# Attention heads with V and the weights split, and the denominators summed on GpSimd

## The reference, cut to what matters

```python
def attend(q, k, v):
    s = jnp.einsum('bqhd,bkhd->bhqk', q, k).astype(jnp.float32) * (MLA_QK ** -0.5)
    p = jax.nn.softmax(s, axis=-1).astype(v.dtype)
    return jnp.einsum('bhqk,bkhd->bqhd', p, v)
# 8 heads, 96 numbers of q and k, 64 of v per head, all float32
# context: 128 queries on their own 128 keys
# latent:  1024 queries on 1024 latent keys and 128 keys of a cache
```

## Time and profile before

| | |
|---|---|
| median of 3 executions | 3778.74 us (3765.2 to 3779.14) |
| the profiled execution | 3774.8 us, its span 3773.0 us |
| PE busy | 3434.7 us, 91% of the span |
| DVE busy | 1973.3 us, 52% |
| ACT busy | 870.4 us, 23% |
| POOL busy | 312.4 us, 8% |
| attention heads of the first layer | about 590 to 961 us of the span |
| attention heads of the second layer | about 2421 to 2793 us |

### The profile page before, as it was taken

The page is one execution under the profiler, slowest core; times in us unless marked ns, Lnnn a source line. Parts: engine busy times, 40 slices in busy tenths (PEclk is TensorE's granted clock), DMA queues, the critical chain, the costliest instruction groups (busy, mean ns, idle before and its releaser), DMA issues. The chain is left out here.

```text
span 3773.0 us, 47227 instructions
## 1 busy us (share of the span) xinstructions
PE 3434.7 (91%) x18786; PEld 3134.0 (83%) x18786; DVE 1973.3 (52%) x3110; ACT 870.4 (23%) x1244; POOL 312.4 (8%) x260
## 2 busy tenths in 40 slices
PE   5985978989979999999989897789998999999998
PEld 4984866666869999999979886566677999999998
DVE  6785535565155665556455755455633543443343
ACT  3112224444231111101131223344432111111100
POOL 1000012221210000000010000212211100000000
PEclk8996568999989999999999966799999999999999
DMA  6500010001112212222121000000011111111011
GB/s 255 159 23 7 16 44 4 2 2 62 45 59 82 79 61 94 73 78 67 45 83 45 28 3 13 4 4 2 11 73 34 45 49 40 44 38 51 33 44 51
DMA packets 44645, 184.32 MB, mean 49 GB/s; under 512 B 5424, under 2 KB 8944, under 8 KB 43120
## 3 DMA queue, kind: packets, MB, share of 16 engines
q1 hardware_dynamic: 37616, 157.53, 11.9%
q0 software_dynamic: 6912, 25.17, 2.3%
HBM read 168.09 MB, written 14.59 MB: 48 GB/s over the span
## 5 line engine op out<-in xcount | busy, mean ns | idle before, releaser
L988 PE MATMUL ps<-a_hi,gu_hi 128*128 128x384 f32 x2112 | 712.0, 337 | 29.8 <-DVE a_lo L1448 23.9
L988 PE MATMUL ps<-a_hi,gu_lo 128*128 128x384 f32 x2112 | 710.2, 336 | 0.0
L988 PE MATMUL ps<-a_lo,gu_hi 128*128 128x384 f32 x2112 | 710.1, 336 | 0.0
L988 PEld LDWEIGHTS ps<-a_hi,gu_hi 128*128 128x128 f32 x2112 | 400.2, 189 | 36.2 <-issue 17.6
L988 PEld LDWEIGHTS ps<-a_lo,gu_hi 128*128 128x128 f32 x2112 | 400.2, 189 | 0.0
L988 PEld LDWEIGHTS ps<-a_hi,gu_lo 128*128 128x128 f32 x2112 | 400.0, 189 | 0.0
L1793 DVE TENSOR_TENSOR at<-ps,sg 128x384 f32<-128x384 f32 x132 | 73.3, 555 | 546.0 <-ACT sg L1320 546.0
L1017 PE MATMUL ps<-g_hi,d_hi 128*128 128x384 f32 x1056 | 354.3, 335 | 4.3 <-DVE g_lo L1795 4.3
L1017 PE MATMUL ps<-g_lo,d_hi 128*128 128x384 f32 x1056 | 354.2, 335 | 0.0
L1017 PE MATMUL ps<-g_hi,d_lo 128*128 128x384 f32 x1056 | 353.9, 335 | 0.0
L909 PE MATMUL ps<-pt,va 128*128 128x512 f32 (+1 forms) x608 | 307.1, 596 | 3.1 <-DVE ya L1726 3.1
(11 more groups left out here) (252 smaller groups left out, 5005.3 us busy)
## 6 DMA issues: line engine op xcount, KB each, us to landing
f_raw<-wgu SPq DMA_DIRECT2D x88, 512.0 KB, 4.6
diag<-wada_c POOLq DMA_DIRECT2D x48, 512.0 KB, 3.8
f_raw<-wdn SPq DMA_DIRECT2D x44, 512.0 KB, 4.6
w_raw<-win SPq DMA_DIRECT2D x32, 512.0 KB, 3.6
wada_z<-wada_b SPq DMA_DIRECT2D x24, 512.0 KB, 4.0
spill<-z SPq DMA_DIRECT2D x2, 4608.0 KB
z<-spill SPq DMA_DIRECT2D x2, 4608.0 KB, 13.7
w_raw<-wout SPq DMA_DIRECT2D x16, 512.0 KB, 3.5
```

Source lines behind the costliest of these rows:

```text
L988: mm = MM(ps[:, 2 * (v % 2) + part, 0:BLK], w, a[:, k, b * BLK:(b + 1) * BLK], start=(k == 0 and j == 0), stop=(k == KC - 1 and j == 2))
```

## The change

The product with V becomes two fp32r matmuls a step. V is split into a high and a low half, which stand side by side as the 128 weight columns: `va` is now [keys, 2, 64]. The exponentials are split too. ACT takes each exponential twice, rounded into `ph` and in f32 into `pf`, and DVE makes `pl` = `pf` - `ph` (`low_weights`). PE multiplies both `ph` and `pl` by `va`. The bank then holds the part from V high in its lower half and that from V low in its upper half. ACT copies the upper half to `t64` (`lower_half`), and DVE adds the two into `tsum`, which keeps two heads, one above the other (`both_halves`).

The ones are gone from `va`. POOL adds up `pf` over the key tiles instead (`accumulate`, 16 additions a head), and once for a pair of heads PE sums over the keys with plain f32 matmuls on ones (`denominators`). DVE inverts them on all 128 partitions (`inverses`, `inverse0`), POOL multiplies (`divided`), ACT rounds (`yhigh`), and POOL makes `a_lo` (`low`).

Further: the context step moves from first to last of the 19; the maxima have no low part any more (`low_rows` and its semaphore are gone); there are 3 max units a step from step 7, where there were 4 from step 6; ACT loads one table that serves the exponential and the logarithm; the low part of V is made on POOL (`low_values`); the residual comes back from HBM in two transfers; and the hardware loops over heads are written out.

```diff
-                MM(ps[:, 6 + (e + o) % 2, 0:n], va[e][:, kt0, :], pt[:, s % 3, 0:n], start=(kt0 <= 1),
+                    pe.wait_ge(at_ph.sem, at_ph.at(l, g + 1))
+                    MM(ps[:, bank, 0:n], va[h % 2][:, kt, :, :], ph[:, g % 3, 0:n], start=first, stop=False)
+                    pe.wait_ge(at_pl.sem, at_pl.at(l, g + 1))
+                    MM(ps[:, bank, 0:n], va[h % 2][:, kt, :, :], pl[:, g % 3, 0:n], start=False,
...
-        S_TRQ, S_TRK, S_PQ, S_PK, S_MAX, S_ROOT, S_ROW = 0, 2, 4, 5, 6, 9, 14
+        S_TRQ, S_TRK, S_VAL, S_PQ, S_PK, S_SUM, S_ROOT, S_INV, S_MAX, S_ROW = 0, 2, 3, 4, 5, 6, 7, 8, 7, 16
...
+                def denominators(h, o, bank):
+                    if o == 2:
+                        pe.wait_ge(at_pf.sem, at_pf.at(l, STEPS * (h + 1)))
+                        sums, dst = [pf0[:, e, :] for e in range(2)], slice(SEQ, 2 * SEQ)
+                    else:
+                        pe.wait_ge(at_acc.sem, at_acc.at(l, 16 * h + 8 * (o + 1)))
+                        sums, dst = [acc[:, e, o, :] for e in range(2)], slice(0, 512)
...
+                    for e in range(2):
+                        mm = MM(ps[DH * e:DH * e + DH, bank, dst], ones[:, 0:DH], sums[e], start=True, stop=True)
...
+                    if h % 2 and st == 13:
+                        denominators(h, 0, o_bank(h, 0))
+                    if h and h % 2 == 0 and st in (3, 4):
+                        denominators(h - 1, 5 - st, o_bank(h - 1, 2))
...
+                        if n == 16 and k == 2:
+                            denominators(H - 1, 2, o_bank(H - 1, 2))
+                            denominators(H - 1, 1, o_bank(H - 1, 1))
...
+                def exponentials(g):
+                    h, st = GLOBAL[g]
+                    n, src = PARTS[at_steps[st][0]][1], 3 + g % 3
+                    act.wait_ge(at_st.sem, at_st.at(l, g + 1))
+                    if g >= 3:
+                        act.wait_ge(at_pv.sem, at_pv.at(l, g - 2))
+                    A(ph[:, g % 3, 0:n], ps[:, src, 0:n], ACT.Exp, scale=SCALE_A).then_inc(at_ph.sem, 1)
...
+                            act.wait_ge(at_acc.sem, at_acc.at(l, acc_after(*GLOBAL[g - 3])))
+                        act.wait_ge(at_pl.sem, at_pl.at(l, max(g - 2, 0)))
...
+                    A(dst, ps[:, src, 0:n], ACT.Exp, scale=SCALE_A).then_inc(at_pf.sem, 1)
...
+                def low_weights(g):
...
+                    TT(pl[:, g % 3, 0:n], src, ph[:, g % 3, 0:n].bitcast(F32), ALU.subtract).then_inc(at_pl.sem, 1)
...
-                    link(V.reciprocal(rec[0:DH, 0:n], ps[DH:P, bank, 0:n]))
-                    TT(ya[half, (e + o) % 2, 0:n], ps[0:DH, bank, 0:n], rec[0:DH, 0:n], ALU.mult).then_inc(at_y.sem, 1)
+                    TT(tsum[half, q0:q0 + n], ps[0:DH, o_bank(h, o), 0:n], t64[0:DH, 0:n], ALU.add).then_inc(at_ts.sem, 1)
...
+                def accumulate(g):
...
+                    pool.wait_ge(at_pf.sem, at_pf.at(l, g + 1))
+                    before = pf[:, (g - 1) % 3, :] if kt == 2 else acc[:, h % 2, o, :]
+                    G.tensor_tensor(acc[:, h % 2, o, :], before, pf[:, g % 3, :], ALU.add).then_inc(at_acc.sem, 1)
...
+                nc.scalar.preload_act_table_set("natural_log_exp_and_others")
```

More of the change, by code:

```diff
@@ new lines, in inverse0, with inverses @@
+                def inverse0(h):
+                    pair = h // 2
+                    dve.wait_ge(at_den.sem, at_den.at(l, 3 * pair + 2))
+                    if pair:
+                        dve.wait_ge(at_ya.sem, at_ya.at(l, 3 * pair - 1))
+                    V.reciprocal(rec0[:, :], ps[:, o_bank(h, 2), SEQ:2 * SEQ]).then_inc(at_rec.sem, 1)
+                def inverses(h, o, bank, first, last):
+                    k = 3 * (h // 2) + (1, 3)[o]
+                    dve.wait_ge(at_den.sem, at_den.at(l, k))
+                    if k > 1:
+                        dve.wait_ge(at_ya.sem, at_ya.at(l, k - 2 if o else k - 1))
+                    for i in range(first, last):
+                        ins = V.reciprocal(rec[:, i * P:(i + 1) * P], ps[:, bank, i * P:(i + 1) * P])
+                    if last == 4:
+                        ins.then_inc(at_rec.sem, 1)
@@ L1743, in _ @@
                 pointwise_low(0)
-                split(0, 0)
+                low_q(0)
+                low_k(0)
                 pointwise_low(1)
-                max_rows(0, 0, True)
-                low_rows(0, 0)
+                for un in range(UNITS):
+                    if un == 6:
+                        sums(1)
+                    if un == 20:
+                        inverse(1)
+                    maximum(0, un)
                 if l == 0:
@@ L1953, in _ @@
                 pool.wait_ge(at_tab.sem, at_tab.at(l, 1))
                 first(0)
+                low_values(0)
                 first(1)
[L1956 to L1962 removed]
@@ L1963, in _ @@
-                head(H - 1, 1, H // 2 - 1, False)
-                pool.wait_ge(at_done.sem, at_done.at(l, 3 * H))
+                pool.wait_ge(ckv_out.sem, ckv_out.at(l, 48))
+                for g, (h, st) in enumerate(GLOBAL):
+                    accumulate(g)
+                    if h + 1 < H and st == 4:
+                        low_values(h + 1)
+                    if h + 2 < H:
+                        if st == 9:
+                            pool.wait_ge(at_rope.sem, at_rope.at(l, h + 2))
+                            normalise_q(h + 2)
+                        if st == 10:
+                            normalise_k(h + 2)
+                        if st == 11:
+                            by_cosine()
+                        if st == 12:
+                            by_sine()
+                        if st == 13:
+                            turned()
+                    if h and h % 2 == 0:
+                        pair = h // 2 - 1
+                        if st == 1:
+                            divided(pair, 0)
+                        if st == 5:
+                            low(pair, 0)
+                        if st == 6:
+                            divided(pair, 2)
+                        if st == 7:
+                            divided(pair, 1)
+                        if st == 14:
+                            low(pair, 2)
+                        if st == 15:
+                            low(pair, 1)
+                    if h == H - 1 and st in (8, 11):
+                        w_low(16 + st // 11)
@@ L1965, in _ @@
+                divided(H // 2 - 1, 0)
+                low(H // 2 - 1, 0)
+                divided(H // 2 - 1, 2)
+                divided(H // 2 - 1, 1)
+                low(H // 2 - 1, 2)
+                low(H // 2 - 1, 1)
                 for n in range(18, 24):
```

509 lines of the change are left out of this document (276 added, 233 removed).

## The result

The changed kernel takes 3852.94 us (median of four, 3851.08 to 3857.84), the kernel before in the same session 3774.69 (four, with the three shown above). The ratio is 1.0213, with a 95% interval of 1.0188 to 1.0237: 78 us slower, where +53 had been forecast. The profiled execution has a span of 3852.8 us against 3773.0.

A forecast was written before the change was run, and what follows sets the result against it. PE was taken to bound the kernel, with DVE taking over in the max-unit steps. Terms of 12 + 5 + 9 + 2 - 1.5 = 26.5 us a layer gave +53 on 3778.7, 3832 us; range 3745 to 3925.

The forecast's parts named there:

- the likeliest case: Whole kernel: DVE's subtractions and POOL's additions collide as forecast, 3832 us, span 3795 to 3865, chance 0.50.
- PE's work falls by 5.4 us a head: Attention heads: cheaper products with V less the added denominators, 87 us over 16 heads if PE stayed the bound.
- DVE becomes the bound of the unit steps: Steps with three max units: subtraction and maxima cost DVE 2.2 us against PE's 1.7 us.
- the walk: Time sum through an odd middle head from its transpose of q: 52.0 us against 50.9 before.
- The collision costs 1.75 us a pair: DVE's subtraction and POOL's addition, both with two SBUF inputs, don't overlap: 1.65 to 1.92 us a pair, taken as 1.75.
- Heads 6 and 7: Last two heads of a layer: 41.4 us against 36.5, and 36.2 against 27.3; +5 and +9 us.
- Heads 0 to 5: Six heads of a layer, odd ones 52.0 us, even ones from 2 on 54.7: 317.4 against 305.2, +12 us.
- The clock rival: More waits in heads bring PE's lower clock: 32 us in all, 3865 us, up to 3925; chance 0.15.
- Denominators: Plain f32 matmuls on PE, 0.87 us per 512 columns: 3.9 us a pair of heads, 2.0 a head.
- The last pair's cover: Output projection's first chunk: seven eighths, some 13 us, cover a chain of about 12; no cost, or a few us.
- No collision: Short DVE and POOL operations slip past each other: 8 us less a layer, 3762 us (3745 to 3785), chance 0.20.
- PE stays the bound: Heads: POOL's additions lag within the buffers, DVE's waits vanish, 87 us of PE work go: 3690 us, chance 0.15.

The follow-up runs named there:

- tiny_both: Changed kernel with POOL's additions and DVE's subtractions both cut to 8 of 512 columns: 3727.07 us, ratio 0.9879.
- psum_sub: Changed kernel with DVE's subtraction reading the scores in PSUM instead of the f32 exponentials in SBUF (result meaningless): 3770.9 us, ratio 0.9992.
- pe_extra: Changed kernel with the first score matmul of steps 7 to 15 of each head done twice: 3856.07 us, ratio 1.0216.
- sum_high: Changed kernel with f32 exponentials written back to PSUM for DVE's subtraction, and POOL summing the rounded exponentials instead: 3773.28 us, ratio 0.9998.
- tiny_inv: Changed kernel with the four reciprocals at the end of heads 3, 5 and 7 cut from 128 to 8 columns: 3854.84 us, ratio 1.0207.
- sums_later: Changed kernel with the sums of squares, their root and inverse, and POOL's following preparation two steps later: 3850.34 us, ratio 1.0202.

## Why the forecast held, and where its sizes were off

3852.94 lies in the likeliest case's own span, 3795 to 3865, in its upper part, and the kernel is slower, as forecast. The mechanism was right. The 3832 is nearer than its parts deserve: six heads were put 22 us a layer too short in the first layer, heads 6 and 7 together 4 us too long. Step by step:

**PE's work falls by 5.4 us a head: the price held, half of the gain could not be had.** The product's two matmuls start 0.23 us apart, as taken; PE in head 2 of after:

```profile
703.39 0.40 PE L959 MATMUL ps<-ph,va 128*128 128x512 f32 x1
703.62 0.40 PE L961 MATMUL ps<-pl,va 128*128 128x512 f32 x1
```

But tiny_both, with the additions and subtractions almost away, gains 46 us of the 87. That the rest stays in the hand-overs between the engines, the chain that the prediction names as the third part of a head, is argued and not shown.

**DVE becomes the bound of the unit steps, at 2.2 us and 2.6 with the collisions: held.** DVE in head 2 of after:

```profile
731.03 1.44 DVE L1782 TENSOR_TENSOR pl<-pf,ph 128x512 fp32r<-128x512 f32 x1
732.39 1.47 DVE L1770 TENSOR_REDUCE pmx<-ps 128x1 f32<-128x384 f32 x3
733.79 0.88 DVE L1782 TENSOR_TENSOR pl<-pf,ph 128x512 fp32r<-128x512 f32 x1
734.59 1.47 DVE L1770 TENSOR_REDUCE pmx<-ps 128x1 f32<-128x384 f32 x3
```

and POOL beside it:

```profile
731.88 2.24 POOL L2019 TENSOR_TENSOR qk<-qk,small 128x960 f32<-128x960 f32 x1
```

Five such steps from 731.03 to 744.09 take 2.61 us each, the forecast's 22 us for 8.3 of them. One piece of this is not the collision: a DVE addition that the walk had left out stands among them.

```profile
735.99 0.67 DVE L1791 TENSOR_TENSOR tsum<-ps,t 64x512 f32<-64x512 f32 x1
```

The subtraction varies between 0.88 and 1.81 us here, as it meets POOL or not; the three maxima, which read PSUM, take 1.47 us whatever POOL does. (The prediction reads this out of the earlier trace rows, but no instruction there has a PSUM input; it is this row and psum_sub that show it.) pe_extra shows the other half: PE had room.

**The collision costs 1.75 us a pair: held at 1.70.** These are head 7's steps. The prediction also weighed the lock that the Trainium skill describes (SBUF — State Buffer, section "SBUF: two separate sides"), by which a pair would cost the sum, 1.92 us. The trace agrees that the two don't overlap, and psum_sub that it ends when one reads PSUM; the size came out 0.22 us lower than that sum.

**Heads 6 and 7: oversized by 4 us (73.6 against 77.6).** Between the marks, head 7 takes 31.1 us where 36.2 was forecast. POOL sets the pace there, with its waits for DVE in it, as its row of instructions without a gap shows. From 973.44 to 1002.4 it does fourteen additions and two low parts of the weights, 29.0 us. Two of the sixteen additions were done before, and the three steps without additions, counted on top at 1.2 us each, lie beside POOL's work.

**Heads 0 to 5: undersized, 339.4 against 317.4.** With sum_high as the kernel without the collision, the miss of 22 us a layer comes apart.
- Without the collision the forecast had 297.2 us for the six, and sum_high takes 306.2: 9 us. They lie in the stretch from the first maxima to the last, put at 18.7 us without the collision: sum_high takes 19.6 to 21.7, 20.5 on the mean. Of the 1.8 us, 0.7 are the `tsum` addition above, which the walk does not have. The way from the transpose of q to the first maxima was 0.9 us shorter than forecast in the odd heads (23.75 against 24.6), from the last maxima to the next transpose 5.6 against 5.4.
- The collision was put at 3.3 us a head, for POOL's preparation pieces alone, because an addition fits beside the maxima. In heads 2 and 4 it costs 2.8 and 2.0 us against sum_high, 3.2 and 2.8 against psum_sub (whose profiled run, at 3762.6 us, is 8 us under its median). That is a little under the forecast.
- In the odd heads it costs 7.2 us on the mean against sum_high, in head 0 6.7. The odd head's walk meets after as follows: first maxima at 24.1 us (forecast 24.6), from there to the last 26.1 to 26.6 (22.0; heads 2 and 4 take 22.5 to 22.7), to the next transpose 7.3 (5.4; heads 2 and 4 take 5.6). The walk has no denominators in an odd head, although the changed kernel does those of the pair's first 512 latent queries there, at step 13, among the max units; what that costs was not tried. The last difference, 1.6 us, is nearly all the row of maxima at the lower clock (below). The clock goes with a part of the rest too: tiny_inv's twins differ by 2.8 us, head 1 of the two layers of after by 2.0. In pe_extra the odd heads, which do 2 us of PE work more, take 55.7 us at 0.94 and 57.6 and 57.0 at 0.91, where after has 57.8 on the mean at 0.85. sums_later has 55.0 at 0.91, but wins there by its own edit too. So 2 to 3 us a head in four heads, some 8 to 12 us a layer, go with the clock, of the 13 that remain.

**The clock rival (0.15) came true in part.** It was put at 2 us a head for stretches at the lower level after new waits. How it looks in head 3 of after, the wait first:

```profile
776.39 0.69 PE L917 MATMUL ps<-kh,qh 96*128 96x384 f32 x1 [4.37 <-DVE pmx L1770]
```

then the stretches around it, and two of some 15 us later:

```profile
772.00:775.00 3.00, 0.02 (x1) 0.00 (x0) 2.64 (x2) 1.30 (x3) 2.46 (x2) 1.00 0.00 0
775.00:778.00 3.00, 1.61 (x4) 1.41 (x5) 2.97 (x7) 1.41 (x4) 1.35 (x2) 0.61 0.00 0
778.00:781.00 3.00, 3.00 (x9) 2.34 (x9) 2.82 (x7) 1.08 (x2) 0.43 (x1) 0.50 0.00 0
790.00:793.00 3.00, 2.79 (x7) 1.85 (x7) 2.90 (x6) 1.09 (x2) 3.00 (x3) 0.50 0.00 0
793.00:796.00 3.00, 3.00 (x8) 0.88 (x7) 2.07 (x4) 0.00 (x0) 3.00 (x4) 0.50 0.00 0
```

PE stands still for 4.37 us, until DVE has sums and first maxima behind it, and then runs at 0.50, the lower of its two levels, 1.2 GHz. In the last stretch its queue holds the pair's denominators, and ACT and DVE wait for it:

```profile
793.84 1.98 PE L976 MATMUL ps<-acc,cst 128*64 128x512 f32 x4
```

The 18 small matmuls that turn the maxima into a row take 3.64 us at 802.56, in head 2 2.13. PE waits for DVE ahead of them and the next product starts behind them, so these 1.5 us are the clock's own. What gives one head further low stretches and its twin none (heads 2 and 4 of tiny_inv) stays open: the wait for the first maxima is much the same (4.66 and 4.70 us in the twins). Nor was it tried whether the odd heads would be shorter with the denominators in another step.

**Denominators: oversized.** Each plain f32 matmul of 512 columns was taken at 0.87 us, two records as in the earlier trace rows. In head 2 of after four records, two such matmuls, take 1.0 us together (the next matmul on PE starts at 712.12), where 1.74 was taken (so PE's work fell by some 0.7 us a head more than the 5.4):

```profile
711.11 1.08 PE L976 MATMUL ps<-acc,cst 128*64 128x512 f32 x4
```

**The last pair's cover held.** PE's first projection matmuls follow head 7 at 1002.61, POOL's last low part ends at 1016.4, and nothing on PE waits for it.

**The other rivals.** "No collision" gave 3762 us for a world that psum_sub and sum_high then made: 3770.9 and 3773.28. "PE stays the bound" had 3690; tiny_both, its nearest kernel, takes 3727. In sum: collision forecast at 70 us (3832 less 3762), measured 82 (after less psum_sub); the rest forecast at -17, measured -2. Part of the clock's loss is in the 82, since it leaves with the collision (0.93 to 0.97 in the heads of psum_sub); how much of the 82 is waiting and how much the clock was not parted.

## What to carry to other kernels

Before work is moved to a second engine to relieve the first, list for both the operations that read two tensors from SBUF; where they are released by the same signal they ran one after the other here, and one operand in PSUM was enough to part them. Read mean durations of the same shape in two kernels, since such waiting is booked as busy time. And price a gain on the busiest engine twice, once by its work and once by the hand-overs with that work taken away: here 87 us of PE work were worth 46 at best.

## What the runs showed of the hardware

- A subtraction of 512 columns on DVE takes 683 ns with one input in PSUM, and 1018 on the mean with both in SBUF beside POOL's additions. The additions take 1277 ns in the first case and 1576 in the second, though nothing of them was changed.
- The denominators' plain f32 matmuls have 64 columns of weights each and go to two halves of PSUM's partitions; two of them, four records, take 1.0 us, where one such matmul of the kernel before, with 128 columns of weights, took 0.87 (priced from the distance between starts). They seem to run side by side; no experiment measured this by itself.
- Two heads with equal instructions differ by 2.8 us with a granted clock of 0.94 or 0.85 (tiny_inv), head 1 of the two layers by 2.0 us with 0.88 or 0.85 (after), and more PE work (pe_extra) went with a higher clock at nearly equal time.
